# Up-projection units of a two-layer trunk: tokens stationary, weights streaming, outputs transposed on TensorE

## The chip, the cores and the metric

The kernel runs on one core of one Trainium2 chip. The metric is the device time of one execution in microseconds (us). Before the change, three runs gave 2182.2, 2182.2 and 2183.59 us; their median is 2182.2 us.

## The reference, cut to what matters

The program is a decoder trunk of two layers for 256 tokens of width 2048, in float32. Layer 0 mixes tokens by a gated unit and a dilated attention, layer 1 by a stick-breaking attention. After the mixer each layer has the same squared-ReLU MLP with a hidden width of 8192:

```python
def squared_relu_mlp(h, w1, w2):
    return jnp.square(jax.nn.relu(h @ w1)) @ w2

# in each layer, after the mixer:
x = x + rmsnorm(y, norm_post_mix[layer])
h = rmsnorm(x, norm_pre_ffn[layer])
y = squared_relu_mlp(h, ffn_w1[layer], ffn_w2[layer])   # (256, 2048) -> (256, 8192) -> (256, 2048)
x = x + rmsnorm(y, norm_post_ffn[layer])
```

The kernel leaves the factor of the root mean square of a token (rmsnorm's scale, `rst[:, 6:8]`, one number for each token) out of the operand of the matmuls and multiplies it in when the product leaves PSUM.

## The kernel before, in words

**Units and ticks.** Every projection is cut into units. A unit multiplies the 256 tokens by a block of 2048 x 512 weights, and there are 94 units in one sequence: 10 and 4 for the mixer of layer 0, 32 for its FFN, then 12, 4 and 32 for layer 1. A unit has eight ticks; a tick takes 256 rows of the weight block (two blocks of 128). All matmuls are in fp32r and in three terms: each operand is split in a high and a low part (`w_hi`, `w_lo`; `act_hi`, `act_lo`, the two halves of `act_pair`; `hid_hi`, `hid_lo`), and hi x hi, hi x lo and lo x hi are summed in PSUM.

**Engines.** SP loads weights in quarters of 1 MB into `w_raw`. ScalarE (`conv`, L357) copies one tick's weights to `w_hi` in a ring of four slots, as soon as TensorE has released the slot by `pe_ticks`; VectorE (`conv`, L652) then writes `w_lo` = `w_raw` - `w_hi`. The loops `unit` of the two engines run these conversions four ticks ahead of TensorE, put `extras` between them at given ticks, and run the unit's `post`, which takes the product out of PSUM, after the seventh. Order on each engine is the order in the code; between engines there are only semaphores. `post_done` counts finished posts, and a TensorE unit u starts when it has reached u - 1.

**Three layouts of a tick.** `tick_tokens` holds 128 tokens stationary and streams 512 columns of weights: 12 matmuls of 512 columns, and the result has tokens in the partitions. `tick_features` holds 128 weight columns stationary and streams the 256 tokens: 24 matmuls of 256 columns, and the result has features in the partitions. `tick_pairs` does the same with high and low part of the tokens streamed in one matmul of 512 columns (8 of them), and 8 of 256 columns for `w_lo`; it fills four PSUM banks whose two halves have to be added.

**The FFN.** The hidden width is done in four groups of 2048. A group has four up units (x times w1) and four down units (hidden times w2, added in `y_sb`). The down units need the hidden block with features in the partitions, as `hid_hi` and `hid_lo`. Before the change the first up unit of a layer is `tick_features` in one PSUM pair, the other fifteen are `tick_pairs` in two sets of four banks; the down units are `tick_tokens`. The post of an up unit: ScalarE copies one half of the four banks (L531), VectorE adds the other (L910), VectorE applies ReLU and the scale in token columns `rs_bc` (L913; L906 in the first unit), ScalarE squares (L534) and copies to `hid_hi` (L536), VectorE subtracts for `hid_lo` (L917).

**The transition into an FFN.** TensorE transposes the new x tile by tile (L1145), ScalarE and VectorE fill `act_pair` (L389, L700), and VectorE sums the squares of x. GpSimd raises them to the power -1/2 (L327, `s_pow`) and then sets `y_sb` to zero (L341). `scale_rows` (L730) spreads the scale over columns, TensorE transposes it in front of the fifth tick of the first unit (L1196), and `scale_tiles` (L736) copies it to `rs_bc`. This goes for fill k = 0 to 3; k = 1 and 3 are the two FFNs, k = 2 is the mixer of layer 1. The output stage of layer 0 has, between its token ticks, transposes of attention weights (L1217).

Of the kernel before, what the change touches and what calls it, by code (L numbers as in the profile page):

```python
# [35 lines left out]
P = 128  # L36
T = 256
# [50 lines left out]
def trunk_kernel(nc, x_in, pre_mix, post_mix, pre_ffn, post_ffn, ab_w_in, ln_g, ln_b, sgu_w, sgu_b,  # L88
                 ab_w_out, sb_w_in, sb_w_out, ffn_w1, ffn_w2, shapes, out):
    ctx = ExitStack()  # L90
    with ctx:
# [49 lines left out]
        relu_t, sq_t = qT, kT  # L141
# [9 lines left out]

        def bank4_halves(par):

            set4 = ps[:, 4 * par:4 * par + 4, :]
            return set4[:, :, 0:T], set4[:, :, T:2 * T]
# [43 lines left out]
        f_rest, f_sum, f_relu, f_sq, f_hi = sem("f_rest"), sem("f_sum"), sem("f_relu"), sem("f_sq"), sem("f_hi")  # L199
# [147 lines left out]
        def _(act):  # L347
# [174 lines left out]
            def ffn(u0, layer):  # L522
                f0 = 16 * layer

                def up(g, jj, par, fresh=False):
                    u, f = u0 + 8 * g + 2 * jj + par, f0 + 4 * g + 2 * jj + par

                    def post():
                        if not fresh:
                            unit_finished(u)  # L530
                            nc.scalar.activation(relu_t[:, :, :], bank4_halves(par)[1], ACT.Copy).then_inc(f_rest, 1)  # L531
                        act.wait_ge(f_relu, f + 1)
                        act.wait_ge(post_done, u)
                        nc.scalar.activation(sq_t[:, :, :], relu_t[:, :, :], ACT.Square).then_inc(f_sq, 1)  # L534
                        act.wait_ge(f_sq, f + 1)
                        nc.scalar.activation(hid_hi[:, bass.ds(8 * jj + 4 * par, 4), :], sq_t[:, :, :], ACT.Copy  # L536
                                             ).then_inc(f_hi, 1)
                    unit(u, post)

                def group_up(g):  # L540
                    with act.Fori(0, 2) as jj:
                        for par in range(2):
                            up(g, jj, par)

                def group_down(g):
                    with act.Fori(0, 2) as jj:
                        for par in range(2):
                            unit(u0 + 8 * g + 4 + 2 * jj + par, nothing)

                for j in range(4):  # L550
                    up(0, j // 2, j % 2, fresh=j == 0)
                group_down(0)
                with act.Fori(1, FGROUPS - 1) as g:
                    group_up(g)
                    group_down(g)
                group_up(FGROUPS - 1)
                total = [junk[:, b * NC:(b + 1) * NC] for b in range(TB)]
                u = u0 + 8 * (FGROUPS - 1) + 4

                def ready(b, j=3):  # L560
                    act.wait_ge(s_ysum, 8 * layer + 2 * j + b + 1)

                for j in range(3):
# [4 lines left out]
                    unit(u + j, post)  # L568
# [70 lines left out]
        def _(dve):  # L639
# [65 lines left out]
            def fill(k, u):  # L705


                for j in range(8):
                    if k == 0 or 1 <= j < 5:
                        conv(u, j)  # L710
                    if k == 0 or j >= 1:
                        evacuate(k, j)
                    if k and j == 5:
                        power = mean_x(k)
                    if k and j == 6:
                        scale_rows(power)
                if k:
                    scale_tiles(k)

# [13 lines left out]
            def scale_tiles(k):  # L733

                dve.wait_ge(s_rt, k + 1)
                nc.vector.tensor_copy(rs_bc[:, :], ps[:, 4, 0:T]).then_inc(s_scales, 1)  # L736
                dve.wait_ge(s_scales, k + 1)
# [159 lines left out]
            def ffn(u0, layer):  # L897
                f0 = 16 * layer

                def up(g, jj, par, fresh=False):  # L900
                    u, f = u0 + 8 * g + 2 * jj + par, f0 + 4 * g + 2 * jj + par

                    def post():
                        unit_finished(u)
                        if fresh:
                            nc.vector.scalar_tensor_tensor(relu_t[:, :, :], bank2_tiles(par), 0.0, rs_tiles,  # L906
                                                           ALU.max, ALU.mult).then_inc(f_relu, 1)
                        else:
# [4 lines left out]
                            nc.vector.scalar_tensor_tensor(relu_t[:, :, :], relu_t[:, :, :], 0.0, rs_tiles,  # L913
                                                           ALU.max, ALU.mult).then_inc(f_relu, 1)
                        dve.wait_ge(f_hi, f + 1)
                        tiles = bass.ds(8 * jj + 4 * par, 4)
                        nc.vector.tensor_tensor(hid_lo[:, tiles, :], sq_t[:, :, :], hid_hi[:, tiles, :].bitcast(F32),  # L917
                                                ALU.subtract).then_inc(post_done, 1)
                    unit(u, post)

                def group_up(g):
                    with dve.Fori(0, 2) as jj:
                        for par in range(2):
                            up(g, jj, par)

                def group_down(g):
                    with dve.Fori(0, 2) as jj:
                        for par in range(2):
                            u = u0 + 8 * g + 4 + 2 * jj + par
                            unit(u, lambda: add_y(u, 2 * NC * jj + NC * par, par).then_inc(post_done, 1))  # L930

                def add_y(u, chunk, par):
                    unit_finished(u)
                    dve.wait_ge(post_done, u)
                    ys = y_sb[:, :, bass.ds(chunk, NC)]
                    return nc.vector.tensor_tensor(ys, ys, bank2(2 * par), ALU.add)

                for j in range(4):
                    up(0, j // 2, j % 2, fresh=j == 0)
# [23 lines left out]
                for j in range(3):  # L963
# [7 lines left out]
                    unit(u3 + j, post)  # L971
# [87 lines left out]
        def _(pe):  # L1059
# [28 lines left out]
            def tick_pairs(par, s, slot, hi, lo, ready):  # L1088


                pe.wait_ge(hi_ready, ready)
                for i in range(2):
                    kt = 2 * s + i
                    for f in range(4):
                        mm(ps[:, 4 * par + f, :], w_hi[:, slot, i, f * P:(f + 1) * P], act_pair[:, kt, :, :],
                           kt == 0, False)
                pe.wait_ge(lo_ready, ready)
                for i in range(2):
                    kt = 2 * s + i
                    for f in range(4):  # L1100
                        last = mm(ps[:, 4 * par + f, 0:T], w_lo[:, slot, i, f * P:(f + 1) * P], hi[:, kt, :],
                                  False, kt == KT - 1)
                last.then_inc(pe_ticks, 1)

# [69 lines left out]
            def late_transposes(k, s):  # L1174
# [15 lines left out]
                if k and s == 4:  # L1190
                    transpose_scales(k)

            def transpose_scales(k):
                pe.wait_ge(s_rep, 2 * (k + 1))
# [102 lines left out]
            def ffn(u0, k):  # L1297
                def up(g):
                    with pe.Fori(0, 2) as jj:
                        for par in range(2):  # L1300
                            unit(u0 + 8 * g + 2 * jj + par, tick_pairs, par)

                def down_pairs(g):
                    with pe.Fori(0, 2) as jj:
                        for par in range(2):
                            down_unit(g, jj, par, 2 * par)

                def down_unit(g, jj, par, buf, closing=False):
                    def hidden_ready(s):
                        if s % 2 == 0:  # L1310
                            pe.wait_ge(post_done, u0 + 8 * g + (s // 2 + 1))
                    unit(u0 + 8 * g + 4 + 2 * jj + par, tick_tokens, buf, hid_hi, hid_lo,
                         before=hidden_ready, closing=closing)


                unit(u0, tick_features, 0, fresh=k)
                pe.wait_ge(s_scales, k + 1)
                for j in range(1, 4):
                    unit(u0 + j, tick_pairs, j % 2)
                down_pairs(0)  # L1320
                with pe.Fori(1, FGROUPS - 1) as g:
                    up(g)
                    down_pairs(g)
                up(FGROUPS - 1)
                for j in range(4):
                    down_unit(FGROUPS - 1, j // 2, j % 2, j % 2, closing=j == 3)
# [83 lines left out]
```

## Time and profile before

| what | value |
|---|---|
| time of the profiled execution | 2182.25 us |
| its span, first to last instruction | 2180.4 us |
| TensorE busy | 2163.5 us, 99% |
| TensorE weight loads | 1891.5 us, 87% |
| VectorE busy | 1236.5 us, 57% |
| ScalarE busy | 1016.1 us, 47% |
| mean granted TensorE clock | 0.999 of full speed |
| traffic with HBM | 186 GB/s over the span |

Busy time is the time in which an engine has an instruction under way. Matmuls are pipelined and their ends are modelled, so the busy share of TensorE does not say how well it is used. A row of the page's groups gives a line and an engine, the tiles written and read, the shapes, the count, and then busy time, mean ns of one, and idle time before it with what ended it.

### The profile page before, as it was taken

To read this page: it belongs to the slowest core of one execution; us is meant where nothing else is said; L and a number is where in the kernel's file an instruction comes from. 1 tells how busy PE (TensorE), PEld (TensorE's weight loads), DVE (VectorE), ACT (ScalarE), POOL (GpSimd) and SP (SyncE) were. 2 spreads that over 40 slices of the span, in tenths; PEclk is the share of its full clock that TensorE was granted. 3 is DMA by queue.
4 is the path that set the end of the run, shared out by engine and by line. 5 is a ranking of instruction groups with operands and counts; after the bars stand their busy time and mean duration, and the time that the engine had idled before them with its cause. 6 is when DMAs were issued, how large, how long until landed. Compare 5 with 4: busy or idle time off the path is not lost.

```text
span 2180.4 us, 30479 instructions
## 1 busy us (share of the span) xinstructions
PE 2163.5 (99%) x12017; PEld 1891.5 (87%) x12017; DVE 1236.5 (57%) x1187; ACT 1016.1 (47%) x1097; POOL 18.7 (1%) x22
## 2 busy tenths in 40 slices
PE   9999999999999999999999999999999999999998
PEld 7999888888888888888899999888888888888886
DVE  5556567555554555555655555566545645554555
ACT  5444345543443443454535545564434534443543
POOL 0000000000000000000000000000000000000000
PEclk9999999999999999999999999999999999999999
DMA  9555555566556556655454555555566565656553
GB/s 310 188 174 174 194 174 156 182 203 193 189 187 191 183 193 212 192 192 193 155 194 155 173 173 188 170 156 184 191 194 192 175 211 174 199 192 210 187 193 116
DMA packets 202768, 406.73 MB, mean 187 GB/s; under 512 B 6400, under 2 KB 7744, under 8 KB 202176
## 3 DMA queue, kind: packets, MB, share of 16 engines
q1 hardware_dynamic: 202272, 405.37, 57.3%
q8 instruction: 59, 0.97, 0.2%
q10 hardware_dynamic: 416, 0.23, 0.0%
q14 instruction: 21, 0.17, 0.0%
HBM read 403.47 MB, written 2.10 MB: 186 GB/s over the span
## 4 chain that ended last, share of the span: by engine, by line
PE 96%; DVE 2%; issue 0%; ACT 0%; DMA 0%; POOL 0%; POOLq 0%; DVEq 0%; SPq 0%; ACTq 0%
PE ps L1061 96%; DVE w_lo L652 1%; DVE act_pair L700 0%; PE ps L1145 0%; DVE tmp L730 0%; DVE x_sb L692 0%; DMA w_raw<-in_ab_w_in_dram 0%; POOL rst L327 0%; ACT act_pair L389 0%; PE ps L1217 0%; ACT tmp L428 0%; ACT w_hi L357 0%; DVE tmp L954 0%; PE ps L1196 0%; DVE bn L995 0%
## 5 line engine op out<-in xcount | busy, mean ns | idle before, releaser
L652 DVE TENSOR_TENSOR w_lo<-w_raw,w_hi 128x1024 fp32r<-128x1024 f32 x752 | 914.2, 1225 | 832.9 <-ACT w_hi L357 822.5
L357 ACT ACTIVATE w_hi<-w_raw 128x1024 fp32r<-128x1024 f32 x752 | 789.6, 1059 | 997.4 <-PE ps L1061 992.0
L1061 PE MATMUL ps<-act_pair,w_hi 128*128 128x256 f32 (+1 forms) x3968 | 854.4, 337 | 0.5 <-issue 0.4
L1061 PEld LDWEIGHTS ps<-act_pair,w_hi 128*128 128x128 f32 x3968 | 664.6, 190 | 64.4 <-issue 1.7
L1061 PE MATMUL ps<-act_pair,w_lo 128*128 128x256 f32 x2944 | 557.4, 283 | 0.0
L1061 PE MATMUL ps<-w_hi,hid_hi 128*128 128x512 f32 x1280 | 499.9, 391 | 0.0
L1061 PE MATMUL ps<-w_hi,hid_lo 128*128 128x512 f32 x1280 | 498.1, 389 | 0.0
L1061 PE MATMUL ps<-w_lo,hid_hi 128*128 128x512 f32 x1280 | 498.0, 389 | 0.0
L1061 PEld LDWEIGHTS ps<-act_pair,w_lo 128*128 128x128 f32 x2944 | 457.6, 191 | 18.7
L1061 PEld LDWEIGHTS ps<-w_hi,hid_lo 128*128 128x128 f32 x1280 | 240.2, 188 | 50.3
L1061 PEld LDWEIGHTS ps<-w_hi,hid_hi 128*128 128x128 f32 x1280 | 240.3, 188 | 49.3
L1061 PEld LDWEIGHTS ps<-w_lo,hid_hi 128*128 128x128 f32 x1280 | 240.4, 188 | 49.1
L1061 PE MATMUL ps<-w_hi,act_pair 128*128 128x512 f32 x512 | 162.1, 392 | 1.5 <-DVE act_pair L700 1.5
L1061 PEld LDWEIGHTS ps<-w_hi,act_pair 128*128 128x128 f32 x512 | 96.1, 188 | 21.4 <-DVE act_pair L700 1.7
L1061 PE MATMUL ps<-w_lo,act_pair 128*128 128x512 f32 x256 | 99.7, 389 | 0.0
L917 DVE TENSOR_TENSOR hid_lo<-kT,hid_hi 128x1024 f32 (+1 forms) x32 | 39.2, 1226 | 76.9 <-ACT hid_hi L536 76.9
L534 ACT ACTIVATE kT<-qT 128x1024 f32<-128x1024 f32 x32 | 33.9, 1060 | 88.0 <-DVE qT L913 83.1
L1061 PEld LDWEIGHTS ps<-w_lo,act_pair 128*128 128x128 f32 x256 | 48.1, 188 | 9.5
L913 DVE SCALAR_TENSOR_TENSOR qT<-qT,rs_bc 128x1024 f32<-128x1024 f32 x30 | 36.7, 1225 | 1.0
L910 DVE TENSOR_TENSOR qT<-ps,qT 128x1024 f32<-128x1024 f32 x30 | 36.5, 1217 | 0.0
L536 ACT ACTIVATE hid_hi<-kT 128x1024 f32 (+1 forms) x32 | 34.0, 1062 | 3.6
L531 ACT ACTIVATE qT<-ps 128x1024 f32<-128x1024 f32 x30 | 30.3, 1010 | 0.0
(108 smaller groups left out, 573.7 us busy)
## 6 DMA issues: line engine op xcount, KB each, us to landing
w_raw<-in_ffn_w_dram SPq DMA_DIRECT2D x256, 1024.0 KB, 5.3
w_raw<-in_sb_w_in_dram SPq DMA_DIRECT2D x48, 1024.0 KB, 5.1
w_raw<-in_ab_w_in_dram SPq DMA_DIRECT2D x39, 1024.0 KB, 5.1
w_raw<-in_ab_w_out_dram SPq DMA_DIRECT2D x16, 1024.0 KB, 5.1
w_raw<-in_sb_w_out_dram SPq DMA_DIRECT2D x16, 1024.0 KB, 5.1
gpost<-in_norm_post_mix_dram SPq DMA_DIRECT2D x2, 1024.0 KB, 7.3
gpost<-in_norm_post_ffn_dram SPq DMA_DIRECT2D x2, 1024.0 KB, 6.8
out_dram<-x_sb SPq DMA_DIRECT2D x3, 512.0 KB, 2.7
```

Source lines behind the costliest of these rows:

```text
L357: nc.scalar.activation(w_hi[:, t % RING, :, :], w_raw[:, t // 2, h:h + 2, :], ACT.Copy).then_inc(hi_ready, 1)
L531: nc.scalar.activation(relu_t[:, :, :], bank4_halves(par)[1], ACT.Copy).then_inc(f_rest, 1)
L534: nc.scalar.activation(sq_t[:, :, :], relu_t[:, :, :], ACT.Square).then_inc(f_sq, 1)
L536: nc.scalar.activation(hid_hi[:, bass.ds(8 * jj + 4 * par, 4), :], sq_t[:, :, :], ACT.Copy).then_inc(f_hi, 1)
L652: nc.vector.tensor_tensor(w_lo[:, t % RING, :, :], w_raw[:, t // 2, h:h + 2, :], w_hi[:, t % RING, :, :].bitcast(F32), ALU.subtract).then_ ...
L910: nc.vector.tensor_tensor(relu_t[:, :, :], bank4_halves(par)[0], relu_t[:, :, :], ALU.add).then_inc(f_sum, 1)
L913: nc.vector.scalar_tensor_tensor(relu_t[:, :, :], relu_t[:, :, :], 0.0, rs_tiles, ALU.max, ALU.mult).then_inc(f_relu, 1)
L917: nc.vector.tensor_tensor(hid_lo[:, tiles, :], sq_t[:, :, :], hid_hi[:, tiles, :].bitcast(F32), ALU.subtract).then_inc(post_done, 1)
L1061: return nc.tensor.matmul(dst, lhsT, rhs, start=start, stop=stop, skip_group_check=True)
```

## The change

All up units become `tick_tokens` in PSUM buffers 0 and 1. Their post applies ReLU and the token's scale with tokens in the partitions (two `tensor_scalar` from PSUM, `rst[:, 6 + b]` as the scale), and ScalarE squares the result into `sq_tok`. In front of the third tick of the next unit TensorE turns `sq_tok` by eight transposes of 128 x 128 into PSUM buffer 2 or 3 (`turn`), ScalarE copies it to `hid_hi` at its tick 3, and VectorE subtracts for `hid_lo` at its tick 4. The fourth unit of a group is turned in the first down unit. The scale in token columns is made for k = 0 and 2 only. The down units use PSUM buffers 0 and 1.

```diff
 # ScalarE
+                def square(f):
+                    act.wait_ge(f_relu, f + 1)
+                    nc.scalar.activation(sq_tok, relu_tok, ACT.Square).then_inc(f_sq, 1)
+
+                def turned_hi(g, j):
+                    act.wait_ge(f_turned, f0 + 4 * g + (j + 1))
+                    nc.scalar.activation(hid_hi[:, 4 * j:4 * j + 4, :], bank2_tiles(2 + j % 2), ACT.Copy
+                                         ).then_inc(f_hi, 1)
...
+                    for j in range(4):
+                        unit(u0 + 8 * g + j, lambda: square(f0 + 4 * g + j),
+                             {3: [lambda: turned_hi(g, j - 1)]} if j else None)
...
 # VectorE, fill
-                    if k and j == 6:
+                    if k == 2 and j == 6:
                         scale_rows(power)
-                if k:
+                if k == 2:
                     scale_tiles(k)
+                elif k:
+                    dve.wait_ge(s_pow, power)
...
 # VectorE, ffn
-                            dve.wait_ge(f_rest, f - layer)
-                            nc.vector.tensor_tensor(relu_t[:, :, :], bank4_halves(par)[0], relu_t[:, :, :], ALU.add
-                                                    ).then_inc(f_sum, 1)
-                            dve.wait_ge(f_sum, f - layer)
-                            nc.vector.scalar_tensor_tensor(relu_t[:, :, :], relu_t[:, :, :], 0.0, rs_tiles,
-                                                           ALU.max, ALU.mult).then_inc(f_relu, 1)
...
+                def relu(g, j):
+                    u, f = u0 + 8 * g + j, f0 + 4 * g + j
+                    unit_finished(u)
+                    for b in range(TB):
+                        last = nc.vector.tensor_scalar(relu_tok[:, b, :], ps[:, 2 * (j % 2) + b, :], 0.0,
+                                                       rst[:, 6 + b:7 + b], ALU.max, ALU.mult)
+                    last.then_inc(f_relu, 1)
+
+                def turned_lo(g, j):
+                    dve.wait_ge(f_hi, f0 + 4 * g + (j + 1))
+                    tiles = slice(4 * j, 4 * j + 4)
+                    nc.vector.tensor_tensor(hid_lo[:, tiles, :], bank2_tiles(2 + j % 2), hid_hi[:, tiles, :].bitcast(F32),
+                                            ALU.subtract).then_inc(post_done, 1)
...
 # TensorE
-                if k and s == 4:
+                if k == 2 and s == 4:
                     transpose_scales(k)
...
+                def turn(g, j):
+
+                    pe.wait_ge(f_sq, f0 + 4 * g + (j + 1))
+                    for b in range(TB):
+                        for f in range(4):
+                            last = nc.tensor.transpose(ps[:, 4 + 2 * (j % 2) + f // 2,
+                                                          (f % 2) * T + b * P:(f % 2) * T + (b + 1) * P],
+                                                       sq_tok[:, b, f * P:(f + 1) * P], ident)
+                    last.then_inc(f_turned, 1)
+
+                def up(g, first=0):
+                    for j in range(first, 4):
+                        unit(u0 + 8 * g + j, tick_tokens, j % 2, extras={2: [lambda: turn(g, j - 1)]} if j else None)
...
-                unit(u0, tick_features, 0, fresh=k)
-                pe.wait_ge(s_scales, k + 1)
-                for j in range(1, 4):
-                    unit(u0 + j, tick_pairs, j % 2)
-                down_pairs(0)
+                f0 = 8 * (k - 1)
+                unit(u0, tick_tokens, 0, fresh=k)
+                up(0, 1)
+                down(0)
```

## Rows read from the trace of the kernel before

**Rows 1.** The page: busy shares, and the chain that ended last by engine.
```profile
PE 2163.5 (99%) x12017; PEld 1891.5 (87%) x12017; DVE 1236.5 (57%) x1187; ACT 1016.1 (47%) x1097; POOL 18.7 (1%) x22
...
PE 96%; DVE 2%; issue 0%; ACT 0%; DMA 0%; POOL 0%; POOLq 0%; DVEq 0%; SPq 0%; ACTq 0%
```

**Rows 2.** Waits: engine, line, waited for: us in total, times, longest us.
```profile
PE ps L1196 <- DVE tmp L730: 3.0, 3, 1.4
```

**Rows 3.** The chain in order of time, FFN of layer 0: start, us, what.
```profile
366.12 689.47 PE ps L1061 x3528
```

**Rows 4.** Timeline of ScalarE, ticks of 24 matmuls: start, us, instruction [idle, releaser].
```profile
369.08 1.06 ACT L357 ACTIVATE w_hi<-w_raw 128x1024 fp32r<-128x1024 f32 x1 [3.59 <-PE ps L1061]
...
377.73 1.06 ACT L357 ACTIVATE w_hi<-w_raw 128x1024 fp32r<-128x1024 f32 x1 [1.82 <-PE ps L1061]
```

**Rows 5.** Timeline, four ticks of a pairs unit, first and last release.
```profile
386.11 1.06 ACT L357 ACTIVATE w_hi<-w_raw 128x1024 fp32r<-128x1024 f32 x1 [0.84 <-PE ps L1061]
...
397.28 1.06 ACT L357 ACTIVATE w_hi<-w_raw 128x1024 fp32r<-128x1024 f32 x1 [1.73 <-PE ps L1061]
```

**Rows 6.** Timeline of ScalarE, five ticks of down units, first and last.
```profile
469.21 1.07 ACT L357 ACTIVATE w_hi<-w_raw 128x1024 fp32r<-128x1024 f32 x1 [1.60 <-PE ps L1061]
...
482.81 1.06 ACT L357 ACTIVATE w_hi<-w_raw 128x1024 fp32r<-128x1024 f32 x1 [1.66 <-PE ps L1061]
```

**Rows 7.** Timeline of ScalarE, a token unit of layer 1's input projection.
```profile
1356.62 1.06 ACT L357 ACTIVATE w_hi<-w_raw 128x1024 fp32r<-128x1024 f32 x1 [1.66 <-PE ps L1061]
1359.34 1.06 ACT L357 ACTIVATE w_hi<-w_raw 128x1024 fp32r<-128x1024 f32 x1 [1.66 <-PE ps L1061]
```

**Rows 8.** The chain in order of time: transposes between matmuls.
```profile
290.24 0.66 PE ps L1217 x6
290.90 2.76 PE ps L1061 x12
293.66 0.66 PE ps L1217 x6
...
1070.53 0.87 PE ps L1145 x8
```

**Rows 9.** Timeline of ScalarE, token ticks with six transposes each between.
```profile
287.62 1.06 ACT L357 ACTIVATE w_hi<-w_raw 128x1024 fp32r<-128x1024 f32 x1 [1.66 <-PE ps L1061]
290.34 1.06 ACT L357 ACTIVATE w_hi<-w_raw 128x1024 fp32r<-128x1024 f32 x1 [1.66 <-PE ps L1061]
...
293.76 1.06 ACT L357 ACTIVATE w_hi<-w_raw 128x1024 fp32r<-128x1024 f32 x1 [1.66 <-PE ps L1061]
...
297.17 1.06 ACT L357 ACTIVATE w_hi<-w_raw 128x1024 fp32r<-128x1024 f32 x1 [1.65 <-PE ps L1061]
```

**Rows 10.** Timeline of all engines at the transition into layer 0's FFN.
```profile
361.97 3.51 POOL L341 MEMSET y_sb<- 128x4096 f32 x1
362.06 3.57 DVE L730 TENSOR_SCALAR tmp<-cst,rst 128x128 f32<-128x128 f32 x2
...
365.55 0.86 DVE L700 SCALAR_TENSOR_TENSOR act_pair<-ps,gpre,act_pair 128x256 fp32r<-128x256 f32 x2
...
365.68 0.44 PE L1196 MATMUL ps<-cst,tmp 128*128 128x128 f32 x2 [1.34 <-DVE tmp L730]
```

**Rows 11.** L730 over the whole run: duration in ns, min, median and max.
```profile
L730 DVE TENSOR_SCALAR tmp<-cst,rst x8: 273/1826/3506, 41.7 to 1472.6; 128x128 f32<-128x128 f32 x8
```

**Rows 12.** Timelines of ScalarE and of VectorE at the end of a token unit.
```profile
1362.12 1.06 ACT L357 ACTIVATE w_hi<-w_raw 128x1024 fp32r<-128x1024 f32 x1 [1.72 <-PE ps L1061]
...
1363.21 1.23 DVE L652 TENSOR_TENSOR w_lo<-w_raw,w_hi 128x1024 fp32r<-128x1024 f32 x1 [1.55 <-ACT w_hi L357]
1364.35 1.40 DVE L860 TENSOR_SCALAR v_sb<-ps,rst 128x512 f32<-128x512 f32 x2
```

**Rows 13.** Timeline, the square of the first up unit and what it follows.
```profile
379.96 1.22 DVE L906 SCALAR_TENSOR_TENSOR qT<-ps,rs_bc 128x1024 f32<-128x1024 f32 x1
...
381.21 1.06 ACT L534 ACTIVATE kT<-qT 128x1024 f32<-128x1024 f32 x1 [2.43 <-DVE qT L906]
```

More of the change, by code:

```diff
@@ L140, in trunk_kernel @@
         gain_rows = tmp[0:4 * KT, HG - 1, 0:P]
-        relu_t, sq_t = qT, kT
+        relu_tok, sq_tok = (t[:, :, :].rearrange("p h t -> p (h t)").rearrange("p (b n) -> p b n", b=TB)
+                            for t in (qT, kT))
         junk = tmp[:, 0:HG, :].rearrange("p h c -> p (h c)")
@@ L198, in trunk_kernel @@
         s_y0 = sem("s_y0")
-        f_rest, f_sum, f_relu, f_sq, f_hi = sem("f_rest"), sem("f_sum"), sem("f_relu"), sem("f_sq"), sem("f_hi")
+        f_relu, f_sq, f_turned, f_hi = sem("f_relu"), sem("f_sq"), sem("f_turned"), sem("f_hi")
         s_scales = sem("s_scales")
@@ L523, in ffn, with first_down @@
                 f0 = 16 * layer
[L525 to L538, printed above, removed]
-                def group_up(g):
-                    with act.Fori(0, 2) as jj:
-                        for par in range(2):
-                            up(g, jj, par)
-                def group_down(g):
[L546 to L551, printed above, removed]
+                def square(f):
[5 more added lines that the diff above has]
+                                         ).then_inc(f_hi, 1)
+                def group_up(g):
+                    for j in range(4):
+                        unit(u0 + 8 * g + j, lambda: square(f0 + 4 * g + j),
+                             {3: [lambda: turned_hi(g, j - 1)]} if j else None)
+                def first_down(g):
+                    return {3: [lambda: turned_hi(g, 3)]}
+                def group_down(g):
+                    unit(u0 + 8 * g + 4, nothing, first_down(g))
+                    with act.Fori(1, 4) as j:
+                        unit(u0 + 8 * g + 4 + j, nothing)
+                group_up(0)
                 group_down(0)
@@ L567, in post @@
                             square_y(total[b], j, b)
-                    unit(u + j, post)
+                    unit(u + j, post, first_down(FGROUPS - 1) if j == 0 else None)
                 for t in range(1, 4):
@@ L733, in scale_tiles @@
             def scale_tiles(k):
-                dve.wait_ge(s_rt, k + 1)
+                dve.wait_ge(s_rt, k // 2 + 1)
                 nc.vector.tensor_copy(rs_bc[:, :], ps[:, 4, 0:T]).then_inc(s_scales, 1)
-                dve.wait_ge(s_scales, k + 1)
+                dve.wait_ge(s_scales, k // 2 + 1)
             def transition(k, u, take):
@@ L921, in group_up @@
-                def group_up(g):
[L922 to L932, printed above, removed]
+                def relu(g, j):
[5 more added lines that the diff above has]
+                    last.then_inc(f_relu, 1)
@@ new lines, in turned_lo @@
+                def turned_lo(g, j):
[3 more added lines that the diff above has]
+                                            ALU.subtract).then_inc(post_done, 1)
+                def group_up(g):
+                    for j in range(4):
+                        unit(u0 + 8 * g + j, lambda: relu(g, j), {4: [lambda: turned_lo(g, j - 1)]} if j else None)
@@ L933, in add_y, with first_down @@
+                def first_down(g):
+                    return {4: [lambda: turned_lo(g, 3)]}
+                def add_y(g, j):
+                    u = u0 + 8 * g + 4 + j
                     unit_finished(u)
                     dve.wait_ge(post_done, u)
[L935 to L939, printed above, removed]
+                    ys = y_sb[:, :, j * NC:(j + 1) * NC]
+                    nc.vector.tensor_tensor(ys, ys, bank2(j % 2), ALU.add).then_inc(post_done, 1)
@@ L940, in ffn, with group_down @@
+                def group_down(g):
+                    for j in range(4):
+                        unit(u0 + 8 * g + 4 + j, lambda: add_y(g, j), first_down(g) if j == 0 else None)
+                group_up(0)
                 dve.wait_ge(s_y0, layer + 1)
@@ L970, in post @@
                         gained(j, 1).then_inc(post_done, 1)
-                    unit(u3 + j, post)
+                    unit(u3 + j, post, first_down(FGROUPS - 1) if j == 0 else None)
                 for t in range(1, 4):
@@ L1086, in tick_features @@
                 last.then_inc(pe_ticks, 1)
[L1088 to L1103, printed above, removed]
             def closing_ticks(buf, u):
@@ L1297, in ffn @@
             def ffn(u0, k):
[L1298 to L1313, printed above, removed]
@@ new lines, in up, with down, hidden_ready @@
+                def up(g, first=0):
+                    for j in range(first, 4):
+                        unit(u0 + 8 * g + j, tick_tokens, j % 2, extras={2: [lambda: turn(g, j - 1)]} if j else None)
+                def down(g, last=False):
+                    for j in range(4):
+                        def hidden_ready(s):
+                            if s % 2 == 0:
+                                pe.wait_ge(post_done, u0 + 8 * g + (s // 2 + 1))
+                        unit(u0 + 8 * g + 4 + j, tick_tokens, j % 2, hid_hi, hid_lo,
+                             extras={2: [lambda: turn(g, 3)]} if j == 0 else None,
+                             before=hidden_ready, closing=last and j == 3)
@@ L1321, in ffn @@
+                f0 = 8 * (k - 1)
+                unit(u0, tick_tokens, 0, fresh=k)
+                up(0, 1)
+                down(0)
                 with pe.Fori(1, FGROUPS - 1) as g:
                     up(g)
-                    down_pairs(g)
+                    down(g)
                 up(FGROUPS - 1)
-                for j in range(4):
-                    down_unit(FGROUPS - 1, j // 2, j % 2, j % 2, closing=j == 3)
+                down(FGROUPS - 1, True)
             pe.wait_ge(s_warm, 1)
```

18 lines of the change are left out of this document (1 added, 17 removed).

## The prediction

> **What bounds the kernel now.** I read the busy shares and the chain that ended last first. TensorE is busy for 2163.5 of 2180.4 us and holds 96% of the chain; VectorE (57%) and ScalarE (47%) are far from full [rows 1]. So a microsecond of TensorE time is a microsecond of the kernel, and work of the other engines counts only where TensorE waits for it. In the list of waits TensorE waits for another engine inside or beside the FFN in one place only: for L730, 3.0 us in three waits [rows 2]. The chain in order of time shows the FFN of layer 0 from its fifth tick on as one unbroken piece of matmuls, 3528 in 689.47 us [rows 3]. The change is therefore first a matter of counting what one tick costs TensorE in each layout.
>
> **What a tick costs in each layout.** ScalarE converts one weight tile a tick, and it starts when TensorE has released the slot, so the distance between two of its L357 rows is TensorE's tick. All three layouts stream 6144 columns in a tick; what differs is in how many instructions.
> - tick_features (24 matmuls of 256): 369.08 to 377.73 us is three ticks, 2.883 us each [rows 4].
> - tick_pairs (8 of 512, 8 of 256): 386.11 to 397.28 is four ticks, 2.793 each [rows 5].
> - tick_tokens (12 of 512): 469.21 to 482.81 is five ticks, 2.720 each, with hid_hi and hid_lo stationary [rows 6]. With act_pair stationary, as the up units will have it, 1356.62 to 1359.34 is 2.72 too [rows 7].
> These three add up to what is there: 4 x 2.883 + 120 x 2.793 + 126 x 2.720 = 689.4 against 689.47 in [rows 3].
>
> By the Trainium skill ("TensorE: Matmul & The Clock Gate", section "Back-to-back issue gap") a warm matmul of N columns takes N / 2.4 + 2.5 ns. That gives 24 x 109.2 = 2.62, 8 x 215.8 + 8 x 109.2 = 2.60 and 12 x 215.8 = 2.59 us for the three ticks, so nearly no gain from fewer instructions (2.9 us in the whole kernel in place of the 20.1 of part 1). The rows disagree: 2.883, 2.793 and 2.720, so here each matmul carries more beside its columns, and I go by the rows.
>
> **Part 1, the up units themselves.** Of the 32 up units, 2 were tick_features (the first of each layer) and 30 tick_pairs. Saved: 30 x 8 x (2.793 - 2.720) = 17.5 us, and 2 x 8 x (2.883 - 2.720) = 2.6 us. Down units keep tick_tokens and only change buffers: 0.
>
> **Part 2, the turns.** Each unit adds 8 transposes of 128 columns between the second and third tick of the next unit, 256 in all, in TensorE's own order, so nothing can lie over them. The chain shows 8 such transposes as 0.87 us at 1070.53 (0.109 each) and six as 0.66 [rows 8]. There is a little more to it: in the output stage of layer 0 six transposes stand between token ticks, and there the tick's distance is 3.42 and 3.41 us (290.34, 293.76, 297.17) against 2.72 without them [rows 9]. That is 0.695 for six, 0.044 more than 6 x 0.1085. Eight then cost at least 0.87, at most 8 x 0.695 / 6 = 0.93; I take 0.87 + 0.044 = 0.91, since a fixed cost at the switch is what the two rows together suggest. 32 x 0.91 = +29.1 us (bounds 27.8 and 29.8).
>
> **Part 3, the transition into each FFN.** The scales in token columns are no longer needed as a broadcast tile, so scale_rows, two transposes (L1196) and the copy L736 go for k = 1 and 3, and stay for k = 2. TensorE stood 1.34 us before L1196, which took 0.44 [rows 10]. Both go: 1.78 x 2 = 3.6 us saved. What is late next? VectorE had L730 twice in 3.57 us there, because GpSimd's memset of y_sb (L341) ran from 361.97 for 3.51 us [rows 10]; the same instruction takes 273 ns at its shortest [rows 11]. In the new order VectorE goes from the last evacuation and the wait on s_pow straight to the conversion for tick 5. That one is a tensor_tensor. If the memset doesn't hold it, it ends near 364.1. Tick 4 now starts near 363.5 (the old tick 3 ended near 364.2, and four ticks are 0.16 shorter each), tick 5 near 366.3: no wait. If the memset holds it too, it ends at 365.5 + 1.23 = 366.7, and TensorE waits 0.4 to 0.5 us, twice: +1 us. With the evacuation before it held as well (0.86) it is 1.3, twice: +2.6.
>
> The Trainium skill ("SBUF — State Buffer", section "Who interferes with whom") says that tensor_scalar in its two-port form and GpSimd exclude each other for a whole instruction, and that an instruction with two SBUF inputs only meets a GpSimd instruction that reads SBUF. L730 beside the memset agrees with the first half; no row here shows the second half, by which the conversion would run free. The sum would be the same 0 that I take.
>
> **Part 4, the posts on VectorE and ScalarE.** A pairs unit cost VectorE three instructions of 1.22 us and ScalarE three of 1.01 to 1.06. Now it is two tensor_scalar of PSUM (1.40 us for both, L860's form [rows 12]) and one subtraction on VectorE, and a square and a copy on ScalarE. That is less work, on engines with slack: 0. What it adds is one chain that TensorE waits for: relu, square, then the turn (wait on f_sq). Take R, the release of the last slot of a unit. In rows 12 R is 1362.12, and the two L860 run from 1364.35 to 1365.75, R + 2.23 to R + 3.63; VectorE does the conversion of that slot before them. A square of this shape follows its input by 0.03 and takes 1.06 [rows 13], so it ends at R + 4.72. The turn comes two ticks after the unit's end, and TensorE's own work begins 0.1 to 0.3 before the row that it releases (transposes at 290.24 in rows 8, ScalarE at 290.34 in rows 9), so at R + 5.44 less that, R + 5.14 to R + 5.34. Slack 0.4 to 0.6 us: no wait. Behind a waiting turn stands all of TensorE's queue, so when that slack is gone each missing tenth costs 3.2 us over 32 units.
> The other new waits have more room. The next conversion on ScalarE stands behind the square and ends at R + 5.8, VectorE's at about R + 7.0; its tick starts near R + 11.6. The last group of tiles is turned in the first down unit: ScalarE's copy comes at its tick 3, VectorE's subtraction at tick 4, ending near R + 15.3, and tick 6 asks for it at about R + 17: 1.7 us to spare. PSUM: up units use buffers 0 and 1, turned tiles 2 and 3, and each is freed a unit ahead.
> DMAs and their order on SP's queue are the same; post_done now counts an up unit half a unit later, and no load of weights waits for it. Loops over units are now written out; the first FFN group was already written out and runs inside the unbroken piece of rows 3: 0.
>
> **Sum.** -17.5 - 2.6 - 3.6 + 29.1 + 0 = +5.4 us. The execution profiled took 2182.25 us (span 2180.4 and 1.85 around it), and the median of the runs is 2182.2, so the forecast is 2187.7 us, 0.25% slower. A difference of 0.2%, 4.4 us, is about what a measurement of this kernel tells from no change; the forecast is only just past it.
>
> **Rivals.**
> - A. The turn waits for the square. For it: the slack is 0.4 to 0.6 us of a chain of 4.7 worked out from rows of other stages. Against it: every piece of the chain has a row. It decides from a chain 0.5 us longer than I have; at 0.8 longer it costs 0.3 x 32 = 10 us, 2197; if the relu fell behind one more conversion (1.22), 0.7 x 32 = 23 us, 2211.
> - B. The memset holds VectorE's conversion (part 3): +1.0 to +2.6 us, 2189 to 2190. For it: L730 in rows 10. Against it: the other form of instruction.
> - C. The other side: a transpose costs less here than its rows. The turn's operands are a different tile, and its price is 256 times one number. The change breaks even where eight cost 23.7 / 32 = 0.74 us, 0.092 each. At half the price, 0.055 each, 14.1 us instead of 27.8, with the same 0.044 at the switch (1.4): -17.5 - 2.6 - 3.6 + 15.5 = -8.2, 2174 us. Against it: transposes of three different tiles take 0.108 to 0.11 each in rows 8.
> By the Trainium skill's formula (same page and section) a transpose of 128 columns would take 55.8 ns, and its gains of 2.9 us in place of 20.1 go with it: -2.9 - 3.6 + 14.3 = +7.8 us. Rows 8 show 0.109, so it is not used.
>
> **How the numbers follow.** Forecast 0.68, its own spread 2185.5 to 2189.5 (turn bounds -1.3 and +0.7, and as much again for the ticks). A 0.17, B alone 0.08, C 0.04, something else 0.03. The range reaches over B and the nearer half of A, and a little below the forecast: 2184.5 to 2195. Slower by over 0.2% (above 2186.6): three quarters of the forecast's case, all of A and B: 0.74. Within 0.2%: 0.21. Faster: C and a part of the rest, 0.05.
>
> **What would show it.** L357 distances of 2.72 in up units and 3.63 (2.72 + 0.91) in the tick with a turn; the groups of transposes unbroken and 0.87 long, with no idle TensorE in front that ends with the square; no L1196 at k = 1 and 3 and the tick after it on time; the L652 beside the memset at 1.23 us. A wait of TensorE for ScalarE's square in most units would show A, an L652 of over 3 us B, transposes closer than 0.1 us C. I am wrong if the token tick in the up units isn't 2.72, since 256 ticks rest on it: a hundredth there is 2.6 us.

## The result, and the profile after

The changed kernel takes 2190.04 us (median of 7 runs, 2189.78 to 2191.78), against 2182.2 before. The ratio is 1.0035, 95% interval 1.0024 to 1.0047: slower by 7.8 us, where 5.4 were forecast. The range of 2184.5 to 2195 holds it. The profiled execution has a span of 2188.2 us, 7.8 more than before. Repeated times of one kernel mostly lie in two groups some 1.5 us apart (2182.1 and 2183.6 us before the change).

The page of the changed kernel first: busy shares, one row of the DMA queues (packets, MB, share), and the chain that ended last by engine. TensorE executes 900 matmuls fewer and is busy 8.2 us longer than in [rows 1]; the instruction queue q8 moved 1.39 MB.
```profile
PE 2171.7 (99%) x11117; PEld 1857.5 (85%) x11117; DVE 1200.6 (55%) x1183; ACT 987.2 (45%) x1067; POOL 18.8 (1%) x22
...
q8 instruction: 85, 1.39, 0.3%
...
PE 98%; DVE 1%; issue 0%; ACT 0%; DMA 0%; POOL 0%; POOLq 0%; DVEq 0%; SPq 0%; ACTq 0%
```

The chain of the changed kernel in order of time (start, us, what). What was one piece of 689.47 us in [rows 3] is now cut by turns (L1273), and by two gaps of a kind that the FFN did not have.
```profile
379.44 0.87 PE ps L1273 x8
380.31 21.79 PE ps L1048 x96
402.10 0.87 PE ps L1273 x8
...
707.68 1.37 issue
709.04 27.51 PE ps L1048 x120
...
1825.70 0.77 issue
1826.47 24.19 PE ps L1048 x106
```
From turn to turn it is 402.10 - 379.44 = 22.66 us; by the first matmuls of the units, those with a turn take 22.65 and 22.69 us in turn, 22.67 in the mean. Eight token ticks are 8 x 2.720 = 21.76, so a turn costs 0.91. The two pieces called issue are time in which TensorE waited for no semaphore. The first lies just at the start of group 2 of layer 0, where TensorE's loop over groups jumps back for its one repeat: ten token ticks and the turn's place (736.55) follow it. The second lies 14 matmuls into group 2 of layer 1.

ScalarE's timeline answers to [rows 4 to 6]. In an up unit of the changed kernel four ticks take 396.75 - 385.87 = 10.88 us, 2.72 each.
```profile
374.10 1.06 ACT L353 ACTIVATE w_hi<-w_raw 128x1024 fp32r<-128x1024 f32 x1 [1.66 <-PE ps L1048]
377.77 1.06 ACT L523 ACTIVATE kT<-qT 128x1024 f32<-128x1024 f32 x1 [2.61 <-DVE qT L898]
...
385.87 1.06 ACT L353 ACTIVATE w_hi<-w_raw 128x1024 fp32r<-128x1024 f32 x1 [0.74 <-PE ps L1048]
...
396.75 1.06 ACT L353 ACTIVATE w_hi<-w_raw 128x1024 fp32r<-128x1024 f32 x1 [1.66 <-PE ps L1048]
```
The same rows carry the chain of the posts. With R = 374.10, the square ends at 378.83, R + 4.73, where R + 4.72 was forecast, and the turn starts at 379.44 in the chain (the record of its first transpose starts at 379.28). That is a slack of 0.45 to 0.6 us, and TensorE waits for no square.

The transition into layer 0's FFN, GpSimd and VectorE (compare [rows 10]). The memset still runs for 3.54 us from 361.27, and three conversions run beside and behind it in 3.51 us. Three in a row took 3.50 us before the change, behind the memset, so it does not hold them.
```profile
361.27 3.54 POOL L337 MEMSET y_sb<- 128x4096 f32 x1
362.03 3.51 DVE L644 TENSOR_TENSOR w_lo<-w_raw,w_hi 128x1024 fp32r<-128x1024 f32 x3
```

The books, by the starts of the units' first matmuls in the two profiles. In the two FFNs the turns are 32 x 0.91 = +29.1 us. The 30 pairs units are -17.7: one took 22.35, and the first unit behind four of them 0.03 more than 21.76. The first unit of each FFN, from its first matmul to the next unit's first, took 26.16 and 26.18 us before and takes 23.24 and 23.24 now, with its ticks and its transition: -5.9. The two gaps cost 1.53 and 0.93 us from start to start of the matmuls around them (1.75 and 1.16 in place of 0.227), and the matmuls behind the first one 0.14 more: +2.6. Together +8.2 in the FFNs (+8.1 by the rounded terms). Outside them the changed kernel's profile is 0.3 us longer behind the start of the last unit, and 0.7 us shorter ahead of the first matmul on weights, which comes at 10.84 us where it came at 11.58. That makes the 7.8 of the spans. The early part is no accident of one profile: that matmul comes at 10.8 to 11.0 us in the seven profiles with the new layout and at 11.2 to 11.6 in the six with the old one. No run here shows why.

### The profile page after: what moved, and what is told of

The parts are those of the page before. It is cut to its first block, busy times and chain, and to the rows that moved or that the text cites. A ratio compares the mean times of both kernels' runs of the same rounds, so it can differ in the third digit from the quotient of the medians.

```text
span 2188.2 us, 28067 instructions
## 1 busy us (share of the span) xinstructions
PE 2171.7 (99%) x11117; PEld 1857.5 (85%) x11117; DVE 1200.6 (55%) x1183; ACT 987.2 (45%) x1067; POOL 18.8 (1%) x22
## 3 DMA queue, kind: packets, MB, share of 16 engines
q8 instruction: 85, 1.39, 0.3%
## 4 chain that ended last, share of the span: by engine, by line
PE 98%; DVE 1%; issue 0%; ACT 0%; DMA 0%; POOL 0%; POOLq 0%; DVEq 0%; SPq 0%; ACTq 0%
PE ps L1048 96%; PE ps L1273 1%; PE ps L1115 1%; DVE w_lo L644 0%; DMA w_raw<-in_ab_w_in_dram 0%; DVE x_sb L684 0%; PE ps L1187 0%; ACT tmp L424 0%; ACT w_hi L353 0%; DVE tmp L941 0%; POOL rst L323 0%; ACT act_pair L385 0%; DVE bn L982 0%; ACT zs L418 0%; PE ps L1317 0%
## 5 line engine op out<-in xcount | busy, mean ns | idle before, releaser
L1048 PE MATMUL ps<-w_hi,act_pair 128*128 128x512 f32 x2560 | 801.6, 391 | 3.8 <-issue 2.1
L1048 PEld LDWEIGHTS ps<-w_hi,act_pair 128*128 128x128 f32 x2560 | 480.6, 188 | 104.0 <-issue 3.7
L1048 PE MATMUL ps<-w_lo,act_pair 128*128 128x512 f32 x1280 | 498.2, 389 | 0.0
L1048 PE MATMUL ps<-act_pair,w_hi 128*128 128x256 f32 x1792 | 326.9, 284 | 0.4 <-issue 0.4
L1048 PEld LDWEIGHTS ps<-w_lo,act_pair 128*128 128x128 f32 x1280 | 240.5, 188 | 48.6
L1048 PEld LDWEIGHTS ps<-act_pair,w_hi 128*128 128x128 f32 x1792 | 279.1, 191 | 1.4 <-issue 0.8
L1048 PE MATMUL ps<-act_pair,w_lo 128*128 128x256 f32 x896 | 253.5, 283 | 0.0
L1048 PEld LDWEIGHTS ps<-act_pair,w_lo 128*128 128x128 f32 x896 | 171.2, 191 | 0.0
L898 DVE TENSOR_SCALAR qT<-ps,rst 128x512 f32<-128x512 f32 x64 | 45.0, 745 | 0.0
L905 DVE TENSOR_TENSOR hid_lo<-ps,hid_hi 128x1024 fp32r<-128x1024 f32 x32 | 39.0, 1218 | 0.0
L1273 PEld LDWEIGHTS ps<-cst,kT 128*128 128x128 f32 x256 | 29.9, 140 | 4.2
L1273 PE MATMUL ps<-cst,kT 128*128 128x128 f32 x256 | 33.2, 272 | 0.0
```

The source lines that it names most:

```text
L898: last = nc.vector.tensor_scalar(relu_tok[:, b, :], ps[:, 2 * (j % 2) + b, :], 0.0, rst[:, 6 + b:7 + b], ALU.max, ALU.mult)
L905: nc.vector.tensor_tensor(hid_lo[:, tiles, :], bank2_tiles(2 + j % 2), hid_hi[:, tiles, :].bitcast(F32), ALU.subtract).then_inc(post_done, 1)
L1048: return nc.tensor.matmul(dst, lhsT, rhs, start=start, stop=stop, skip_group_check=True)
L1273: last = nc.tensor.transpose(ps[:, 4 + 2 * (j % 2) + f // 2, (f % 2) * T + b * P:(f % 2) * T + (b + 1) * P], sq_tok[:, b, f * P:(f + 1) * ...
```

## The experiments

Eleven kernels, each timed beside the kernel before, whose medians there are 2182.15 to 2182.24 us. The differences told are between medians unless a profile's span is named.

### E1: the jump back taken out of the changed kernel

```diff
-                with pe.Fori(1, FGROUPS - 1) as g:
+                for g in range(1, FGROUPS - 1):
```


> The changed kernel (2190.0 us) with TensorE's loop over FFN groups 1 and 2 written out, so that no jump back is left in its FFN. Theory: the two gaps of TensorE at the start of group 2 of each layer (1.37 and 0.77 us of idle time put down to issue) come from the jump back in a body of eight written-out units; they go, with the few slow matmuls behind them: 2.4 us less, 2187.6 us, and no gap over 0.5 us inside either FFN. Rival: the gaps come with the place in the program or with the longer code as such; then they stay or move, and the time stays at 2190.

Measured: 2187.65 us (ratio to before 1.0023, 1.0014 to 1.0032), 2.4 us less than the changed kernel. Neither FFN has a start-to-start distance of matmuls over 0.5 us. So the gaps come with the jump back, not with longer code as such: with both groups written out, TensorE's code is longer still.

### E2: the long body alone, in the old layout

```diff
                 def up(g):
-                    with pe.Fori(0, 2) as jj:
+                    for jj in range(2):
...
                 def down_pairs(g):
-                    with pe.Fori(0, 2) as jj:
+                    for jj in range(2):
```


> The kernel before (2182.2 us) with only TensorE's inner loops over pairs of units written out, so that the loop over groups has a body of eight units as in the changed kernel; same instructions otherwise. Theory (the long body alone makes the gap): one gap of about 1 us at the start of group 2 of each layer, 2184.0 to 2184.8 us. Rival (the gap belongs to the new layout, as my forecast had it that writing out is free): no gap, 2182.2.

Measured: 2185.68 us (ratio 1.0016, 1.0007 to 1.0025), 3.5 us more than before. TensorE's timeline in E2 has two gaps by issue, one at the start of group 2 of layer 0 and one late in the first tick of group 2 of layer 1.
```profile
708.21 0.96 PE L1061 MATMUL ps<-act_pair,w_hi 128*128 128x512 f32 x3 [0.41 <-issue]
```
```profile
1823.47 0.62 PE L1061 MATMUL ps<-act_pair,w_lo 128*128 128x256 f32 x3 [2.16 <-issue]
```
From start to start they are 0.80 us behind a matmul of 512 columns (0.227 without the gap) and 2.44 behind one of 256 (0.12). So they cost 0.58 and 2.32 us, 2.9 in all, and the slower matmuls behind them 0.2 more, which makes the 3.1 us between the profiled spans. That is more than expected. The layout is the old one, so the long body is enough for them. The kernel before jumps back in the same outer loop, with short inner loops in it, and has no gap there. But a long body does not make a gap at each jump: E5 below has the changed kernel's loop and none in layer 0.

That the sequencer has to fetch the body again is a likely reason; the runs show the jump and the length, not the fetch. The instruction queue's bytes do not settle it: it moved 0.97 MB before and 1.39 MB after, but 1.29 MB in E1, which has no gap. The rows of the kernel before and of E1:
```profile
q8 instruction: 59, 0.97, 0.2%
```
```profile
q8 instruction: 79, 1.29, 0.2%
```

### E3: the memset held back in the kernel before

```diff
+                pool.wait_ge(f_relu, 16 * layer + 1)
                 nc.gpsimd.memset(y_sb[:, :, :], 0.0).then_inc(s_y0, 1)
```


> The kernel before (2182.2 us) with GpSimd's memset of y_sb held back until the first ReLU of the FFN. Theory: the memset alone held L730 for 3.2 us; L730 then takes about 0.3 us each as at k = 2, TensorE's wait of 1.34 us before L1196 goes at k = 1 and 3, and 2.7 us of the 3.6 us that I credited to the change's transition are the memset's: 2179.5 us. Rival: L730 is slow at k = 1 and 3 for another reason (the writes beside it, the wait on the power): it stays at 3.4 us and the time at 2182.

Measured: 2179.06 us (ratio 0.9986, 0.9977 to 0.9995), 3.1 us less. The instruction that was L730 (duration in ns, min, median and max over eight):
```profile
L731 DVE TENSOR_SCALAR tmp<-cst,rst x8: 272/280/288, 41.8 to 1471.1; 128x128 f32<-128x128 f32 x8
```
Against 273/1826/3506 in [rows 11], so the memset was the whole of it. By the Trainium skill ("SBUF — State Buffer", section "Who interferes with whom") a VectorE instruction in a two-port form and a GpSimd instruction exclude each other for the length of an instruction. E3 agrees, 3506 ns at most with the memset beside it and 288 without; that L730 runs in that form is inferred. The second half of that rule, that an instruction with two SBUF inputs is not held by a GpSimd instruction that only writes, agrees with the changed kernel's three conversions above. TensorE's wait of 1.34 us is gone, and of the 1.78 the 0.22 us of the two transposes are left, as the chain of E3 shows:
```profile
358.64 5.76 PE ps L1062 x48
364.40 0.22 PE ps L1197 x2
```
The first units take 24.61 us in both layers, where they took 26.16 and 26.18.

### E4: fewer changes of length in the pairs tick

```diff
+                if s % 2:
+                    pe.wait_ge(lo_ready, ready)
+                    low(False)
+                    last = high(True)
+                else:
+                    pe.wait_ge(hi_ready, ready)
+                    high(False)
+                    pe.wait_ge(lo_ready, ready)
+                    last = low(True)
```


> The kernel before (2182.2 us) with the order inside every second tick of tick_pairs turned round (w_lo first, then w_hi), same matmuls. Theory: a stream of 512-column matmuls that follows shorter ones loses about 0.03 us over its first five (0.228 to 0.236 instead of 0.2267 us each); such a change of length then comes once in two ticks instead of once in one, so 240 x 0.5 x 0.032 = 3.8 us less, 2178.4 us. Rival: the 512-column matmuls of a pairs tick are slower because each goes to another PSUM bank than the one ahead: no change of the order cures that, 2182.

Measured: 2181.24 us in the median (ratio 0.9991, 0.9982 to 1.0), and 2179.47 to 2182.69: this kernel falls in the later group of times more often than the one before, and group against group it is 2.6 us faster (2179.5 against 2182.1). The profiled span is 2177.6 us, 2.8 less; 2.4 of it lie in the FFNs, and the rest ahead of the first matmul on weights, which the edit does not touch. The ticks are now 2.76 and 2.80 in turn, 2.78 in the mean against 2.793 (ScalarE's timeline in E4):
```profile
410.80 1.06 ACT L357 ACTIVATE w_hi<-w_raw 128x1024 fp32r<-128x1024 f32 x1 [1.39 <-PE ps L1061]
413.56 1.06 ACT L357 ACTIVATE w_hi<-w_raw 128x1024 fp32r<-128x1024 f32 x1 [1.71 <-PE ps L1061]
416.36 1.06 ACT L357 ACTIVATE w_hi<-w_raw 128x1024 fp32r<-128x1024 f32 x1 [1.74 <-PE ps L1061]
```
The 512-column matmuls of the pairs units fell from 0.2300 to 0.2284 us in the mean, half of the way to 0.2267, as the theory has it. That is 3.1 us over 1920 of them; about 0.8 us came back on the shorter ones. Right in kind, too large in size: 3.8 us were expected.

### E5: every turn twice

```diff
-                    for b in range(TB):
+                    for b in (0, 1, 0, 1):
```


> The changed kernel (2190.0 us) with every turn done twice, 16 transposes in place of 8 into the same PSUM tiles, nothing else. Theory: a turn is 8 x 0.1085 us of TensorE's own time and about 0.04 at the switch, and the second eight cost no further switch: 32 x 0.868 = 27.8 us more, 2217.8 us. Rival: what a turn costs is largely fixed (a wait or a switch), the transposes themselves lie partly over the matmuls: clearly under 20 us more.

Measured: 2217.06 us (ratio 1.0159), 27.0 more than the changed kernel. The chain of E5:
```profile
404.56 1.75 PE ps L1273 x16
406.31 21.81 PE ps L1048 x96
428.12 1.75 PE ps L1273 x16
```
Sixteen transposes are 1.75 us, eight were 0.87, and the 96 matmuls between keep their time. E5 has one loop gap of 1.23 us, in layer 1, where the changed kernel has 2.5 us in two, so its doubling cost 28.2 us, 0.110 for a transpose. No part of it lies over other work. That excludes rival C, which needed 0.092.

### E6: the turn in two halves

```diff
-extras={2: [lambda: turn(g, j - 1)]} if j else None
+extras={2: [lambda: turn(g, j - 1, 0)], 3: [lambda: turn(g, j - 1, 1)]} if j else None
```


> The changed kernel (2190.0 us) with each turn in two parts of four transposes, before the third and before the fourth tick. Same instructions, one more change from short to long matmuls a unit. Theory: each such change costs 0.04 us, 32 x 0.04 = 1.3 us more, 2191.3 us. Rival: the cost beside the transposes is per transpose or belongs to the wait, no difference: 2190.0.

Measured: 2191.65 us (ratio 1.0043), 1.6 more than the changed kernel, 0.05 for each further break (a unit takes 22.73 us, not 22.67). The chain of E6 shows where: the tick behind a break takes 2.77.
```profile
402.28 0.44 PE ps L1274 x4
402.72 2.77 PE ps L1048 x12
405.49 0.44 PE ps L1274 x4
```

### E7: the scale in token columns made again

```diff
-                    if k == 2 and j == 6:
+                    if k and j == 6:
                         scale_rows(power)
...
-                if k == 2 and s == 4:
+                if k and s == 4:
                     transpose_scales(k)
```


> The changed kernel (2190.0 us) with one part undone: the scale in token columns is made again at k = 1 and 3 (scale_rows, two transposes, the copy), though nobody reads it. Theory: that part was worth 1.8 us a transition, 3.6 us in all: 2193.6 us, and L730 takes 3.4 us beside the memset again. Rival: TensorE would have come late anyway, below 1 us: 2190 to 2191.

Measured: 2196.58 us (ratio 1.0068), 6.5 more than the changed kernel in the median; the profiled spans differ by 5.5 (2193.7 and 2188.2). The waits of TensorE in E7 (us in total, times, longest):
```profile
PE ps L1164 <- DVE tmp L722: 4.0, 3, 1.9
```
The longest is 1.9 us, 1.4 in [rows 2]. The scale arrives when it did, but the four ticks ahead of it are shorter now, and the wait takes that up. The first unit takes 25.60 and 25.58 us instead of 23.24: 4.7 us. The rest of the 5.5 is the loop gaps, 3.2 us here in place of 2.5. The median is 1.1 us above the profiled execution, which is the lowest of five; no profile shows that part. Theory and rival were both too small. The part is worth 4.7 us when it is undone last, and 3.6 by the rows when it is taken first: the four ticks ahead of the wait are 0.16 us shorter each, and the wait grows by as much.

### E8: the turn one tick earlier

```diff
-extras={2: [lambda: turn(g, j - 1)]} if j else None
+extras={1: [lambda: turn(g, j - 1)]} if j else None
```


> The changed kernel (2190.0 us) with the turn before the second tick of the next unit, not the third. It measures the slack of the chain relu, square, turn. Theory: the turn's place comes 2.72 us earlier, the slack was about 0.5 us, so TensorE waits 2.1 to 2.3 us for the square in each of 32 units: 67 to 74 us more, 2257 to 2264 us. Rival: the chain is shorter than its rows say, or its engines come earlier when TensorE waits: under 60 us more.

Measured: 2295.03 us (two executions, 2293.5 and 2296.56; ratio 1.0517, 1.0497 to 1.0536), 105 more than the changed kernel. TensorE's wait in the timeline, and in the list of waits:
```profile
570.98 1.10 PE L1273 MATMUL ps<-cst,kT 128*128 128x128 f32 x8 [2.16 <-ACT kT L523]
```
```profile
PE ps L1273 <- ACT kT L523: 69.1, 32, 2.2
```
The waits are as expected, 2.16 us each. A unit with such a wait and the full clock takes 25.06 us where it took 22.67: 2.39 lost, 76.5 us in all, which puts the slack at 0.3 to 0.6 us (2.72 less 2.39 or 2.16). The remaining 30 us were in neither theory. They are the clock, below.

### E9: the two small gains together

Both edits, of E3 and E4, in the kernel before.

> The kernel before (2182.2 us) with both small changes that helped by themselves: the memset held back until the first ReLU (2179.1 us) and the turned order in every second pairs tick (its profiled span was 2.8 us shorter). Theory: they touch different places and add, 2182.2 - 3.1 - 2.8 = 2176.3 us in the lower group of its times. Rival: the shorter ticks bring the scales' wait back, and the gain stays under 4 us: 2178 or more.

Measured: 2176.68 us (ratio 0.9976, 0.9966 to 0.9985). That is 5.6 us less than before and 13.4 less than the changed kernel: the fastest version of this study.

### E10: long and short matmuls in turns

```diff
+                        mm(ps[:, 4 * par + f, :], w_hi[...], act_pair[:, kt, :, :], ...)
+                        last = mm(ps[:, 4 * par + f, 0:T], w_lo[...], hi[:, kt, :], ...)
```


> The kernel before (2182.2 us) with 512- and 256-column matmuls of a pairs tick in turns (w_hi, w_lo, w_hi, w_lo, ...), same matmuls, and one wait on lo_ready at the start of a tick. Theory (a change of length costs): eight changes a tick; if each cost the 0.03 us of a whole run of matmuls it would be up to 7 x 0.03 x 240 = 50 us more, at the least some microseconds. Rival (only the count of matmuls counts, 8 x 0.2267 + 8 x 0.12 = 2.774 a tick): 240 x 0.019 = 4.6 us less.

Measured: 2190.22 us (ratio 1.0035), 8.0 more than before, and the tick is 2.827 us (ScalarE's timeline in E10, 414.54 to 423.02, three ticks):
```profile
414.54 1.06 ACT L357 ACTIVATE w_hi<-w_raw 128x1024 fp32r<-128x1024 f32 x1 [1.56 <-PE ps L1061]
...
423.02 1.06 ACT L357 ACTIVATE w_hi<-w_raw 128x1024 fp32r<-128x1024 f32 x1 [1.77 <-PE ps L1061]
```
Only counting matmuls (2.774) is excluded. But eight changes cost 0.053 us together, 0.007 each, where one a tick costs 0.019: a change costs more after a run of short ones. My price of 0.03 for each was wrong here.

### E11: another PSUM bank for every matmul

```diff
-                    for b in range(TB):
+                    for term in range(3):
+                        for b in range(TB):
```


> The changed kernel (2190.0 us) with tick_tokens in another order: the three terms outside, the two blocks of tokens inside, so that every matmul goes to another PSUM bank than the one before it, as in tick_pairs. Theory: the bank does not matter, 0.2267 us a matmul, 2190.0 us. Rival (the 0.004 us that a 512-column matmul of a pairs tick costs more is the price of changing banks): some 6400 matmuls x 0.004 = 26 us more, 2216 us.

Measured: 2189.95 us (ratio 1.0035), no difference from the changed kernel. The bank is not the reason.

## Why the prediction was right, step by step

- **TensorE bounds the kernel, so count ticks.** Right. All terms in the FFNs are TensorE's matmuls, transposes, waits and gaps.
- **Part 1, ticks.** Right: 2.72 in the up units, as forecast; the pairs units gave 17.7 us of a forecast 17.5.
- **Part 2, turns.** Right: 0.91 forecast, 0.91 measured. E5 and E6 show its two parts, 0.110 for a transpose and 0.04 (0.91 less 8 x 0.109) to 0.06 at the break. (Against rival C the prediction named three tiles at 0.108 to 0.11; [rows 8] show two, L1217's and L1145's.)
- **Part 3, the transition.** The first units gained 2.92 and 2.94 us; forecast was 1.78 for the transition and 1.3 for the ticks, 3.1 each. The memset doesn't hold the conversion: rival B is out. E3 adds what the prediction left open: 1.55 us of each needed no change of layout, since only the memset's place cost it. What the new layout itself gave is the ticks.
- **Part 4, the posts.** Right: slack 0.45 to 0.6 us, no wait. Rival A did not come; E8 shows its price, and the price was higher than I worked out, since long waits lower the clock too.
- **Part 4, "Loops over units are now written out ... 0".** Wrong, and nearly the whole miss. I looked at the first group, which stood outside the loop before and ran without a gap. But code outside the loop says nothing on a jump back. The jump back in a body of eight written-out units costs 0.9 to 1.5 us in the changed kernel, once a layer, 2.5 us in all (E1: -2.4; E2: +3.5 from the long body alone). With it the sum is 7.9, and without it E1 stands at 2187.65 where the forecast was 2187.7. That this fits to a tenth is partly luck: the 0.7 us of the program's start had no term, and the first units, the pairs units and the end, each 0.2 to 0.3 us off, make up for much of it.

The formula of the Trainium skill ("TensorE: Matmul & The Clock Gate", section "Back-to-back issue gap"), which the page gives for an isolated matmul, made +7.8 us, the measured number, from two wrong terms. It has a transpose at 0.056 us and E5 shows 0.110, which leaves out some 15 us; it has the gain of the ticks at 2.9 us and the traces show 20.3, which leaves out 17. The 2.6 us by which these two do not cancel happen to be what the loop gaps cost. A sum that agrees is no proof of its terms.

## What to carry to other kernels

Where one engine holds the chain, price a change of layout by the spacing of whole ticks read from the trace, not by columns: here 12, 16 and 24 instructions for the same 6144 columns took 2.72, 2.79 and 2.88 us. A transpose on that engine is paid in full, and 0.91 us a unit was more than the 0.59 that the better layout gave. Look at the jump back of a loop whose body grows, and look for cheap waits (a memset in the wrong place) before a change of layout takes the credit for them.

## What the runs showed of the hardware

**A wait of 2.16 us can cost more than itself.** E8's TensorE waits 32 times for 2.16 us. After some of these waits the granted clock falls to 0.50 (1.2 GHz), after others it stays at 1.00 (2.4 GHz). Three stretches of E8: columns are us, then busy us and count of PE, PEld, DVE, ACT and POOL, the granted clock, DMA share and GB/s.
```profile
370.00:379.00 9.00, 6.84 (x31) 5.33 (x31) 4.81 (x5) 3.29 (x4) 0.00 (x0) 1.00 0.67 193
379.60:382.80 3.20, 3.20 (x11) 2.71 (x10) 1.22 (x1) 0.23 (x1) 0.00 (x0) 0.50 0.55 209
383.00:393.00 10.00, 10.00 (x46) 8.28 (x45) 4.43 (x4) 4.45 (x5) 0.00 (x0) 1.00 0.36 105
```
The first holds the wait, in the second token matmuls start 0.43 us apart instead of 0.227. The trace has 19 such stretches between the start and the end of the program's work. The units with a turn take 26.65 us with such a stretch and 25.06 without, so each costs 1.6 us, the 30 us that the waits leave over. Right behind each wait stand the eight transposes of a turn; no run here tells whether the wait alone lowers the clock.

**The two groups of times.** The profiled execution of E5 was one of the later group (2218.7 us, others at 2216.9), and it has one such stretch in the first tick of the program:
```profile
11.20:14.40 3.20, 3.20 (x9) 2.48 (x8) 2.09 (x4) 1.46 (x3) 0.00 (x0) 0.50 1.04 403
```
The profiles of E1 and E9, also of the later group (1.5 and 1.4 us above the rest of their times), have it in the same place. That of E10 stands 3.0 us above the rest and is at the lower clock for twice as long:
```profile
11.00:17.60 6.60, 5.98 (x16) 4.72 (x17) 3.81 (x6) 2.39 (x4) 0.00 (x0) 0.50 1.04 396
```
The other nine profiles have none there. So in these profiles the two groups differ by this stretch, at 1.4 to 1.8 us each; why it comes in some executions and not in others is open.

**A change of length costs.** Matmuls of 512 columns right behind shorter ones start 0.228 to 0.236 us apart, then 0.2267 again: for about five of them behind 256-column matmuls, for about nine behind a turn. The price of a change depends on what ran ahead (E4, E6, E10), and not on the PSUM bank (E11). Why is open.
